# Written-out experts with the ring's slots in turn, combination products moved, and a tenth weight tile in four arena pieces

## What is computed

```
def expert_choice_ffn(h, w_router, w_gate, w_up, w_down):
    cap = max(1, (EC_CAPACITY * n) // N_EXPERTS)              # 32
    aff = jax.nn.softmax((h @ w_router).astype(jnp.float32), axis=-1)
    g, idx = lax.top_k(jnp.swapaxes(aff, 1, 2), cap)
    xe = jax.vmap(lambda hb, ib: hb[ib])(h, idx)
    a = jnp.einsum('becd,edf->becf', xe, w_gate)
    up = jnp.einsum('becd,edf->becf', xe, w_up)
    y = jnp.einsum('becf,efd->becd', jax.nn.silu(a) * up, w_down) * g[..., None]
    return zeros.at[idx].add(y)                               # per token
```

## Time and profile before

| | us |
|---|---|
| median of 3 runs | 2744.36 (2743.35 to 2745.78) |
| the profiled execution | 2746.78 |
| its span in the profile | 2745.0 |
| mean granted TensorE clock | 0.99 of full speed |

### The profile page before, as it was taken

How to read it: one execution, slowest core, us unless ns; L and a number is a source line. 1 busy time by engine, 2 the same in 40 slices (tenths; PEclk the granted TensorE clock), 3 DMA queues, 4 the chain that set the end, 5 groups by cost and what they waited for, 6 DMA issues and landing times.

```text
span 2745.0 us, 33174 instructions
## 1 busy us (share of the span) xinstructions
PE 2536.9 (92%) x12537; PEld 1678.3 (61%) x12537; DVE 1403.9 (51%) x2437; ACT 1012.0 (37%) x1890; POOL 32.3 (1%) x45
## 2 busy tenths in 40 slices
PE   8999997777899999877789999999999999999999
PEld 5666432222465553322237788877888988887887
DVE  4988200001276530000124788668887468975776
ACT  5224111001121421000004656566565456655544
POOL 0000000000000000000000000000000000000000
PEclk9999999999999999999999999999999999999999
DMA  8767799999965369999994487616866418863242
GB/s 353 316 286 278 332 380 426 427 426 428 426 253 240 154 251 426 427 425 427 427 425 204 179 338 279 250 62 253 328 259 275 184 71 327 312 249 127 95 188 100
DMA packets 65268, 796.95 MB, mean 290 GB/s; under 512 B 9276, under 2 KB 10556, under 8 KB 15484
## 3 DMA queue, kind: packets, MB, share of 16 engines
q1 hardware_dynamic: 61424, 790.65, 70.3%
q10 hardware_dynamic: 3724, 4.66, 0.5%
HBM read 794.23 MB, written 1.05 MB: 290 GB/s over the span
## 4 chain that ended last, share of the span: by engine, by line
PE 70%; DMA 19%; DVE 7%; ACT 2%; issue 2%; SPq 0%; ACTq 0%; DVEq 0%
PE banks L2305 12%; PE banks L2316 9%; PE banks L1682 7%; DMA ring<-in_t_up 6%; DMA ring<-in_t_down 6%; PE banks L994 6%; DMA ring<-in_t_gate 6%; PE banks L1007 5%; PE banks L1702 5%; PE banks L2318 4%; PE banks L1761 3%; PE banks L1904 1%; PE banks L749 1%; PE banks L2028 1%; PE banks L871 1%
## 5 line engine op out<-in xcount | busy, mean ns | idle before, releaser
L1682 PE MATMUL banks<-ring,arena 128*64 128x512 f32 x1904 | 432.4, 600 | 84.5 <-DMA ring<-in_t_gate 45.3
L3054 DVE TENSOR_TENSOR arena<-arena,banks 128x512 f32<-128x512 f32 x32 | 22.0, 687 | 757.2 <-PE banks L1682 757.2
L2316 PE MATMUL banks<-u_pair,w_hi 128*128 128x512 f32 x1024 | 362.8, 399 | 1.7 <-DVE u_pair L1284 1.7
L3601 DVE TENSOR_TENSOR ring_lo<-ring,w_hi 128x1024 fp32r<-128x1024 f32 x256 | 311.8, 1220 | 99.1 <-ACT w_hi L2816 97.3
L1682 PEld LDWEIGHTS banks<-ring,arena 128*64 128x64 f32 x1904 | 138.9, 137 | 364.6 <-issue 263.3
L2816 ACT CAST w_hi<-ring 128x1024 fp32r<-128x1024 f32 x256 | 267.6, 1050 | 197.0 <-PE banks L2305 139.9
L2318 PE MATMUL banks<-u_pair,ring_lo 128*128 128x256 f32 x1024 | 287.6, 281 | 0.0
L2465 ACT COPY arena<-banks 32x512 f32<-32x512 f32 (+1 forms) x96 | 55.3, 576 | 499.1 <-PE banks L1702 498.2
L1702 PE MATMUL banks<-ring,arena 128*64 128x512 f32 x896 | 206.1, 608 | 28.3 <-DVE arena L3056 10.5
L2316 PEld LDWEIGHTS banks<-u_pair,w_hi 128*128 128x128 f32 x1024 | 192.4, 188 | 51.3 <-ACT arena L1254 3.7
L2305 PE MATMUL banks<-w_hi,ffn_h_hi 128*128 128x512 f32 x512 | 199.4, 389 | 0.0
(11 more groups left out here) (420 smaller groups left out, 4162.9 us busy)
## 6 DMA issues: line engine op xcount, KB each, us to landing
ring<-in_t_ffn SPq DMA_DIRECT2D x64, 2048.0 KB, 8.1
ring<-in_t_gate SPq DMA_DIRECT2D x60, 2048.0 KB, 29.4
ring<-in_t_ada_dots SPq DMA_DIRECT2D x54, 2048.0 KB, 9.7
ring<-in_t_down SPq DMA_DIRECT2D x48, 2048.0 KB, 28.6
ring<-in_t_up SPq DMA_DIRECT2D x43, 2048.0 KB, 30.3
ring<-in_t_ada SPq DMA_DIRECT2D x18, 2048.0 KB, 17.1
ring<-in_t_up SPq DMA_DIRECT2D x32, 1024.0 KB, 28.5
ring<-in_t_ret_in SPq DMA_DIRECT2D x12, 2048.0 KB, 8.0
```

Source lines behind the costliest of these rows:

```text
L1682: mm = nc.tensor.matmul(PS[64 * h:64 * h + 64, f.bank, :], x, wview(u, 4)[:, k % 4, h * 512:(h + 1) * 512], start=(k == 0), stop=(k == KC ...
L2316: nc.tensor.matmul(PS[:, f.bank, :], hi[:, q, :], u_pair[:, q].rearrange("p s t -> p (s t)"), start=(q == 0), stop=False, skip_group_check ...
L3601: TT(w_lo, w, w_hi[:, n % 4].bitcast(F32), ALU.subtract).then_inc(S("ffn_w_lo"), 1)
```

## The change

Slots are taken in turn through a stage, and the last expert alone is sent in parts. In the second stage tile 8 goes to four places of the arena (a slot of its own, sent after tile 9). All experts are written out on TensorE, SyncE and VectorE and read `moe_xe`; for one set, two neighbours' tokens are multiplied together and the right half of the rows is taken. `x_cur` and all of GpSimd's part (`moe_pool`) go. VectorE makes all of `moe_lo`, after each second selection, and the first gather does all eight products of `moe_hi` before those of `moe_lo`. Experts from 4 on use banks 0 to 3 alone. `weigh` for groups 0, 1, 2, 3 stands after experts 9, 10, 12, 15, and set 0's products for groups 0, 1, 2 inside experts 10, 11 and 13, four ahead of each of their four tiles. The four constant DMAs go from ScalarE's queue to SyncE's, behind the fourth `in_t_ada_dots` tile.

```diff
@@ plan_moe
-            order = [n % n_slots for n in range(24 - 24 % n_slots)]
-            order += [n + (2 if n_slots == RING else 1) for n in range(24 % n_slots)]
...
+            units = [(SLOT, (lambda it, e=e, w=w, h=h: w[e, h])) for e in range(E)
+                     for w in (a["t_gate"][l], a["t_up"][l], a["t_down"][l]) for h in range(2)]
+            at, sent, cleared = [slots[n % n_slots] for n in range(96)], None, plan["cd_out"][-1] if l else plan["ab_out"][-1]
+            once = RING + 2 if l else RING
+            at = at[0:8] + [once] + at[8:95]
+            sent = [n for n in range(n_slots + 1) if n != 8] + [8] + list(range(n_slots + 1, 96)) if l else \
+                list(range(7)) + [8, 7] + list(range(9, 96))
+            us = load(at, units, sent=sent)
+            if l:
+                us[8].parts = [Mark(S(f"apart{i}"), 16) for i in range(3)] + [us[8].landed]
+                us[8].places = (10240, 11264, 18432, 20480)
+            for slot in (RING, RING + 1, RING + 2):
+                if slot in at:
+                    us[at.index(slot)].after = plan[p + "norm"][0].full if slot == RING + 2 else cleared.full
...
-            fs = fills(p + "experts", [0, 1, 2, 3, 4, 5, 6, 7] * 2, 3, first=1)
+            fs = fills(p + "experts", [0, 1, 2, 3] * 4, 3, first=1)
...
+            for n, parts in ((2, 2), (3, 2), (5, 4)):
+                u = us[6 * (E - 1) + n]
+                u.parts = [Mark(S(f"piece{n}_{i}"), 16 * (l + 1)) for i in range(parts - 1)] + [u.landed]
-            fills(p + "combine", [0, 1, 2, 3, 4, 5, 6, 7][:4 * ns])
+            fills(p + "combine", [4, 5, 6, 7, 0, 1, 2, 3][:4 * ns])
@@ SyncE
+                if u.places:
+                    for i, part in enumerate(u.parts):
+                        sp.dma_start(wchunk(u, i), shape[:, i * D:i * D + D]).then_inc(part.sem, 16)
+                    return
...
+            def hyena_constants():
+                plan["moe0_combine"][-1].full.wait(sp)
+                sp.dma_start(hy_const, a["k_hyena"]).then_inc(S("hy_const"), 16)
+                sp.dma_start(hf_w1[0:33, :], a["hf_w1"][0]).then_inc(S("hy_const"), 16)
...
+                    if u is plan["hy_const_behind"]:
+                        hyena_constants()
@@ TensorE, gather
-                        for k0 in (0, 4):
+                        span = KC if half == 0 and s == 0 else 4
+                        for k0 in range(0, KC, span):
@@ TensorE, experts
-                def expert_pe(j, it, first=False, beside=None):
...
-                    if not first:
-                        pe.wait_ge(S("x_cur"), 12 * l + j - 3 + it * 4)
+                def expert_pe(e):
+
+                    beside = {10: 0, 11: 1, 13: 2}.get(e)
+                    if beside is not None:
+                        pe.wait_ge(S("y_lo"), 8 * l + ns * beside + 1)
...
+                    cs = slice(e % 8, e % 8 + 1) if ns == 2 else slice(e % 8 - e % 2, e % 8 - e % 2 + 2)
...
-                                beside(h0 + k // 4)
+                                combine(0, h0 + k // 4, (beside,))
...
-                                x = x_cur[:, b, k, :]
+                            x = moe_xe[l][:, e // 8, k, cs].rearrange("p e s c -> p (e s c)")
...
-                with pe.Fori(1, 3) as it:
-                    for j in range(4):
-                        expert_pe(j, it)
-                for j in range(3):
-                    expert_pe(j, 3)
...
-                expert_pe(3, 3, beside=early)
+                for e in range(E):
+                    expert_pe(e)
+                    if 1 <= e <= ns:
+                        gather(1, [e - 1])
@@ ScalarE
-                            r = 64 * h + 32 * s
+                            r = 64 * h + 32 * (s if ns == 2 else j % 2)
...
-                plan["moe0_combine"][-1].full.wait(act)
-                act.dma_start(hy_const, a["k_hyena"]).then_inc(S("hy_const"), 16)
-                act.dma_start(hf_w1[0:33, :], a["hf_w1"][0]).then_inc(S("hy_const"), 16)
-                act.dma_start(hf_w2[0:64, :], a["hf_w2"][0]).then_inc(S("hy_const"), 16)
-                act.dma_start(hf_w3[0:64, :], a["hf_w3"][0]).then_inc(S("hy_const"), 16)
@@ VectorE
-                    if t == 3:
-                        for r in (2, 3):
+                    if t % 2:
+                        for r in (t - 1, t):
                             dve.wait_ge(S("moe_hi"), 4 * l + r + 1)
                             TT(moe_lo[l][:, r, :], moe_utok[l][:, r, :], moe_hi[:, r, :].bitcast(F32), ALU.subtract)\
-                                .then_inc(S("moe_lo_late"), 1)
+                                .then_inc(S("moe_lo"), 1)
...
-                with dve.Fori(1, 3) as it:
-                    for j in range(4):
-                        expert_dve(j, it)
+                for j in range(4):
+                    expert_dve(j, 1)
+                for j in range(4):
+                    expert_dve(j, 2)
+                    if 1 <= j <= 2:
+                        weigh(j - 1)
                 for j in range(4):
                     expert_dve(j, 3)
-                    weigh(j)
+                    if j in (0, 3):
+                        weigh(2 + j // 3)
@@ GpSimd
-            def moe_pool(l, ns):
...
-                for r in range(TC):
-                    pool.wait_ge(S("moe_hi"), 4 * l + r + 1)
-                    nc.gpsimd.tensor_tensor(moe_lo[l][:, r, :], moe_utok[l][:, r, :], moe_hi[:, r, :].bitcast(F32),
-                                            ALU.subtract).then_inc(S("moe_lo"), 1)
...
-                def put_x(j, part):
-                    nc.gpsimd.tensor_copy(x_cur[:, j % 2, :, 0:CAP * ns].rearrange("p k (s c) -> p k s c", s=ns), part)\
-                        .then_inc(S("x_cur"), 1)
...
```

More of the change, by code:

```diff
@@ L253, in __init__ @@
         self.landed = Mark(landed, 16 * (before + 1), 16 * step)
-        self.used, self.after, self.parts = None, None, []
+        self.used, self.after, self.parts, self.places = None, None, [], None
 class Quarter:
@@ L363, in block_program @@
         bank_free = [sem(f"bank_free{b}") for b in range(8)]
-        landed = [sem(f"landed{s}") for s in range(RING + 2)]
+        landed = [sem(f"landed{s}") for s in range(RING + 3)]
         sems = {}
@@ L390, in fills, with load @@
             return got
-        def load(slots, sources, rounds=1, looped=True, first=0, sent=None):
+        def load(slots, sources, rounds=1, looped=True, sent=None):
             per = {s: slots.count(s) for s in set(slots)}
@@ L402, in load @@
                 slot_uses[s] += per[s] * rounds
-            stream.append((rounds, looped, first, [got[n] for n in sent] if sent else got))
+            stream.append((rounds, looped, [got[n] for n in sent] if sent else got))
             return got
@@ L480, in plan_moe @@
             f0 = f0 + fills(p + "expert3", [4, 5, 6, 7])
-            fs = fills(p + "experts", [0, 1, 2, 3, 4, 5, 6, 7] * 2, 3, first=1)
-            for some, banks in ((u0, f0), (us, fs)):
-                for j in range(4):
[L484 to L492, removed]
-            fills(p + "combine", [0, 1, 2, 3, 4, 5, 6, 7][:4 * ns])
+            fs = fills(p + "experts", [0, 1, 2, 3] * 4, 3, first=1)
+            for e in range(E):
+                g, u, t, d = (fs if e >= 4 else f0)[4 * (e % 4):4 * (e % 4) + 4]
+                for i, f in enumerate((g, u, d)):
+                    us[6 * e + 2 * i].used = Mark(S("moe_half"), 48 * l + 3 * e + i + 1)
+                    us[6 * e + 2 * i + 1].used = f.full.in_round(e // 4)
+            plan[p + "first"], plan[p + "units"] = f0, us
+            for n, parts in ((2, 2), (3, 2), (5, 4)):
+                u = us[6 * (E - 1) + n]
+                u.parts = [Mark(S(f"piece{n}_{i}"), 16 * (l + 1)) for i in range(parts - 1)] + [u.landed]
+            fills(p + "combine", [4, 5, 6, 7, 0, 1, 2, 3][:4 * ns])
         def use_dense(name, units, per_unit, banks):
@@ L1461, in send @@
                 sp.dma_start(dst, shape).then_inc(u.landed.sem, 16)
-            for rounds, looped, first, units in stream:
+            def hyena_constants():
+                plan["moe0_combine"][-1].full.wait(sp)
+                sp.dma_start(hy_const, a["k_hyena"]).then_inc(S("hy_const"), 16)
+                sp.dma_start(hf_w1[0:33, :], a["hf_w1"][0]).then_inc(S("hy_const"), 16)
+                sp.dma_start(hf_w2[0:64, :], a["hf_w2"][0]).then_inc(S("hy_const"), 16)
+                sp.dma_start(hf_w3[0:64, :], a["hf_w3"][0]).then_inc(S("hy_const"), 16)
+            for rounds, looped, units in stream:
                 for u in units:
                     w = users.get(u.slot)
-                    send(u, first, ([w] if w else []) + ([(u.after, 0)] if u.after else []))
-                    users[u.slot] = (u.used, first)
+                    send(u, 0, ([w] if w else []) + ([(u.after, 0)] if u.after else []))
+                    users[u.slot] = (u.used, 0)
+                    if u is plan["hy_const_behind"]:
```

(7 more changed lines are left out.)

110 lines of the change are left out of this document (36 added, 74 removed).

## The result

The changed kernel takes **2718.84 us**, the median of 4 runs (2717.0 to 2721.48), against 2745.02 for the kernel before beside it (4 runs, 2743.35 to 2745.78): a ratio of 0.9906 with a 95% interval of 0.9889 to 0.9923. That is 26.2 us less. The forecast was 2718.2, also 26.2 less. The profiled execution was the slowest of the four, 2721.48 us with a span of 2719.7.

The account below looks back on a forecast made before the run. The weight stream was taken to set the expert stages, the engines the rest. Gains of 13.8 us in the first stage, 12.4 in the second and 0 at the constants make 26.2: 2744.4 to 2718.2 us, own range 2713 to 2723.

Parts of the forecast that it names:

- Part 1: First stage's experts: slots in turn end the stream's stall from 350 to 390 us, -7.6 us.
- Part 2: Both stages' experts: parts sent for the last expert only, three rounds less at 0.2 us each, -0.4 and -0.6 us.
- Part 3: Second stage: a tenth tile sent while the stream stands still leaves one fewer in the bound part, -4.9 us.
- Part 4: Both stages' starts: VectorE no longer waits for GpSimd's subtractions, clock loss in the gathers goes, -4.2 and -3.4 us.
- The clock terms: First gathers of both stages: with the running sum sooner, TensorE doesn't idle and its clock holds, -0.9 and -1.7 us.
- Part 5: Both stages' ends: combination products leave the last expert, lag after the last tile falls to 2.2 us, -1.6 and -3.5.
- Part 6: After the first stage: constants' sends leave the chain, 1.5 us, but a wait of 1 to 1.5 returns it: 0.
- Part 7: Remaining edits, such as `x_cur` gone, half the banks, written-out code and moved `weigh`: 0, under 6 us of slack an expert.
- Rival A: Both starts: the running sum is as slow by itself, so 7.6 us falls away, 2725.8 to 2727 us; chance 0.15.
- C: Expert stages: slots in turn still leave the stream waiting for TensorE, about 2726 us; chance 0.06.
- B: A stream term fails: stall returns later, tenth tile too late, or constants 3 us late; 2721 to 2726 us; chance 0.12.
- D: Expert stages: the stream's pace falls with pieces and constants in one queue; 2765 us at 405 GB/s; chance 0.03.

Follow-up runs that it names:

- after_again: Second profiled execution of the changed kernel, no edit: 2718.78 us, ratio 0.9916 to the kernel before.
- later groups: Two later groups of runs, the unedited changed kernel against the kernel before: 2718.78 against 2741.30 us and 2717.89 against 2742.63 us.

## Why the prediction was right

The number was right for its reasons, and it missed in three sizes.

- **What bounds it, the frame of the sum.** Right. Each part that gave the stream back some time came out one for one in the stage, and what follows took it over: 1299.2 before, 1298.4 in after_again.
- **Part 1, slots in turn: -7.6.** 7.5 measured.
- **Part 2, parts in the last expert only: -0.4 and -0.6.** 1.3 and 1.25 for three rounds each (0.6 to 1.3 and 0.9 to 1.4 against all profiles with these stages untouched), inside the bounds but **too small by about half**. The row I took, 425 against 427, held one round with parts in 25 us; the rate was read to a whole GB/s, which at this size is half of the term. Stretches of 400 us would have told it better.
- **Part 3, tenth tile: -4.9.** 5.0 measured. The trace also settles the page weighed against it. Without the tile the prefill is through at about 980.1, 1.4 us earlier than in the changed kernel, as its sends are (963.41 against 964.77); there it would be through at 981.5 and goes on to 986.6, so the four pieces took about 5.1 us. By the estimate from the Trainium skill (DMA: Bandwidth & Descriptors, "Anatomy of one DMA") they needed 12.8. The measurement decides: pieces queued behind one another did not pay that page's fixed cost each.
- **Part 4, start: -4.2 and -3.4.** -4.2 and -3.2. Split by the run with GpSimd: 2.03 for the sum and 0.36 for the subtractions in the second stage (forecast 2.1 and 0.4). The clock terms, 0.9 and 1.7, hold against the one execution they were read from; in the run with GpSimd the loss came in the first stage (5.3 in all) and not in the second (1.7). Without GpSimd's subtractions no start lost anything to the clock: all eleven profiles have 16.25 to 16.27 and 11.81 to 11.83 us.
- **Part 5, end: -1.6 and -3.5.** The mechanism was right: after the change the last down product starts on its second-last tile, and its 7.09 us end the stage. But the products alone are worth 2.3 and 2.0. **The term that was mis-sized is the second stage's**: I took the whole of the lag of 5.7 for theirs, when only 2.0 comes back with them. Most of the rest stands in the earlier trace rows: the same 16 products take 5.35 us at 1400.79 and 3.65 at 713.05, 1.7 more, and this is the clock in that one execution of the kernel before:

```profile
1400.00:1405.00 5.00, 4.21 (x12) 1.32 (x14) 0.00 (x0) 0.00 (x0) 0.00 (x0) 0.66 1.01 429
...
1400.79 5.38 PE banks L1682 x16
```

The first line is a stretch (columns as in the earlier trace rows, the clock at 0.66), the second is from the chain. From there on the chain of waits holds only TensorE's own work and short steps of other engines, no tile, to the end of the stage. So the 1.7 stayed in the lag, and as an estimate 5.7 is 2.2 of down, 1.7 of slow clock and 1.8 of products. The step that failed beside it is a silent one, that TensorE would run the last down product at full clock. In 7 of 18 stage ends without products in the last expert the clock fell and the product took 1.4 to 1.7 us longer. That took back 1.69 + 1.48 = 3.2 us of this part's 5.1 in the first profile; the stretches outside the two stages, net 3.1 us shorter there (4.1 - 3.3 + 1.3 + 1.1), covered it in the total. I had taken the clock out where it was slow before and priced no slow clock after. That moving the products away is what lets it fall isn't shown.
- **Part 6, constants: 0.** 0.4 us less in after_again, 1.3 less in the first profile, where the end came 1.7 us later and no wait was left. The 1.5 for the sends was nearer to 1.0, and the wait of 1 to 1.5 measured 0.8.
- **Part 7, nothing.** No sign of another term, but none of its items was put back alone. The second stage's -9.1 is less than 5.0 + 1.25 + 2.0 and the 1.7 of slow clock before, 9.95 in all.
- **In the first stage the parts do not add up.** Put back one at a time they cost 7.5 + 1.3 + 2.3 = 11.1, together 9.3. Whether the old stall and the old end cover one another by 1.8 us wasn't tried; the kernel before is the only one with all three.

Rival A fell with GpSimd's run, C with the old slots, B with both of its runs. D, a slower pace, is refuted by 427 GB/s over 400 us in both stages. That the gain agrees to a tenth of a us is luck: the errors of single parts cancel, runs of one kernel differ by 4 us, and the gain was 22.5 and 24.7 us in the later groups. The steps were also sized on one slow execution of the kernel before, 2746.78 us at a granted clock of 0.991; others took down to 2739.49, at 0.995. As an estimate from its rows, 0.9 + 1.7 in the starts and 1.7 at the second stage's end, 4.3 of the 26.2 us were slow clock of that execution.

## What to carry to other kernels

Where a weight stream sets a stage, count it in tiles and slots: here one use of slots out of turn cost 7.5 us, and a tile sent into an idle gap was worth its transfer, 5.0 for 4.9. Where an operation ends the same half microsecond behind another engine's operation twice, suspect a wait, and move the other engine's work to test it: here it gave all of 2.0 us back. Before a lag is put down to one cause, compare the durations of like groups within it, since 1.7 us of this one was a slow clock; and settle parts under 1 us by their stretch of the trace, since the clock in untouched code moves the total by several.

## What the runs showed of the hardware that I had not expected

- The granted clock varies between executions in code that is the same: the first affinity copy comes at 260.11 to 264.81 us, and the stretch between the stages takes 214.4 to 217.8. Each is as large as a part of this change.
- The same waits of TensorE in the last expert (its last down product waited 1.7 us for its tile in the first profile, 1.6 in the second) were followed by a fall of the clock in one execution and by none in the other. So these waits don't decide whether the clock falls in the product.
- The compare of one input and the running sum of two were held alike by GpSimd's subtraction in the first stage, 2.28 and 2.71 us; in the second stage the compare took 0.33. It began at 992.71, 0.2 before the first of the two equal subtractions was over (990.53 + 2.36). In both stages it ended 0.15 us behind that subtraction (270.81 and 270.67; 993.04 and 992.89).
- With filling products between its tiles, TensorE lost little or nothing on the stream: 443.01 and 432.96 us of experts, 443.18 and 433.10 with the constants earlier, against 442.4 to 443.1 and 433.1 to 433.5.
